# A fused two-block kernel on one core: the first stage rebuilt, top-k rounds and index pairs moved

## The reference, cut to what matters

```python
def gmlp_spatial_gating(h, w_in, ln_g, ln_b, w_s, b_s, w_out):
    uv = jax.nn.gelu(h @ w_in)                  # h is rms_norm(x); w_in 1024 x 2048
    u, v = jnp.split(uv, 2, axis=-1)
    v = layer_norm(v, ln_g, ln_b)
    v = v.reshape(bsz, nblk, 128, 8, 128)       # 4 blocks of 128 tokens, 8 channel groups
    w_masked = jnp.where(mask[None], w_s, 0)    # per group 128 x 128
    sv = jnp.einsum('gij,bnjgd->bnigd', w_masked, v)
    sv = sv + jnp.transpose(b_s)[None, None, :, :, None]
    return (u * sv.reshape(...)) @ w_out
...
    rel = jax.nn.relu(jnp.einsum('bqhd,bsd->bqhs', qib, k_idx32))     # 8 index heads
    score = jnp.einsum('bqhs,bqh->bqs', rel, wb)
    score = jnp.where(admissible[None], score, NEG_BIG)
    top_val, top_pos = lax.top_k(score, n_sel)                        # 128 of up to 512 keys
```

## Time and profile before, and how to read it

| what | value |
|---|---|
| median of 3 runs | 2488.84 us |
| profiled execution | 2489.14 us |
| its span, first to last instruction | 2487.0 us |
| PE busy | 2386.9 us (96%) |
| DVE, ACT, POOL busy | 1349.9, 811.8, 303.8 us |
| chain that ended last | PE 86%, DVE 9%, ACT 3%, issue 2% |
| one ACT pass over 128x512 fp32 | 0.63 us, with a gain 0.71 us |
| one DVE pass over 128x512 fp32 | 0.68 to 0.75 us, GpSimd silent |

### The profile page before, as it was taken

How to read it: one execution, slowest core, us unless ns; L and a number is a source line. 1 busy time by engine, 2 the same in 40 slices (tenths; PEclk the granted TensorE clock), 3 DMA queues, 4 the chain that set the end, 5 groups by cost and what they waited for, 6 DMA issues and landing times.

```text
span 2487.0 us, 28963 instructions
## 1 busy us (share of the span) xinstructions
PE 2386.9 (96%) x10924; PEld 1929.7 (78%) x10924; DVE 1349.9 (54%) x1983; ACT 811.8 (33%) x1274; POOL 303.8 (12%) x139
## 2 busy tenths in 40 slices
PE   6789999999999999999999999998999999999997
PEld 4677888887767788888788888767877888888886
DVE  5566444346566644434655445788664454444455
ACT  2113333233455433323322223330244343222233
POOL 6670000000000000000000000556540000000000
PEclk8899999999999999999999999999999999999999
DMA  4222433331223243333233333223212343333221
GB/s 171 68 85 68 119 95 99 94 101 52 75 75 100 62 124 95 93 101 98 61 100 110 93 93 94 60 68 95 67 56 62 95 130 95 107 93 102 79 79 55
DMA packets 64833, 221.94 MB, mean 89 GB/s; under 512 B 7504, under 2 KB 9680, under 8 KB 64592
## 3 DMA queue, kind: packets, MB, share of 16 engines
q1 hardware_dynamic: 59184, 208.17, 28.1%
q10 hardware_dynamic: 5536, 12.19, 1.6%
HBM read 218.23 MB, written 2.10 MB: 89 GB/s over the span
## 4 chain that ended last, share of the span: by engine, by line
PE 86%; DVE 9%; ACT 3%; issue 2%; DMA 0%; POOL 0%; ACTq 0%; DVEq 0%; POOLq 0%
PE PS L445 23%; PE PS L447 22%; PE PS L446 22%; PE PS L464 3%; PE PS L541 2%; PE PS L515 2%; PE PS L468 1%; PE PS L694 1%; DVE MK L1745 1%; PE PS L715 1%; DVE SS L1372 1%; DVE TOP L1744 1%; PE PS L704 1%; PE PS L840 1%; DVE WL L1360 1%
## 5 line engine op out<-in xcount | busy, mean ns | idle before, releaser
L445 PE MATMUL PS<-XH,WH 128*128 128x512 f32 x1632 | 647.5, 397 | 17.4 <-DVE T L1570 12.5
L447 PE MATMUL PS<-XH,WL 128*128 128x512 f32 x1632 | 637.2, 390 | 0.0
L446 PE MATMUL PS<-XL,WH 128*128 128x512 f32 x1632 | 636.8, 390 | 0.0
L1360 DVE TENSOR_TENSOR WL<-RAW,WH 128x1024 fp32r<-128x1024 f32 (+1 forms) x336 | 396.3, 1180 | 232.4 <-ACT WH L990 227.8
L990 ACT ACTIVATE WH<-RAW 128x1024 fp32r<-128x1024 f32 (+2 forms) x340 | 344.6, 1014 | 350.3 <-DVE M L1477 202.4
L445 PEld LDWEIGHTS PS<-XH,WH 128*128 128x128 f32 x1632 | 307.4, 188 | 99.4 <-issue 20.9
L445 PE MATMUL PS<-HH,WH 128*128 128x512 f32 x928 | 364.1, 392 | 2.6 <-DVE HL L1446 2.6
L447 PE MATMUL PS<-HH,WL 128*128 128x512 f32 x928 | 361.4, 389 | 0.0
L446 PE MATMUL PS<-HL,WH 128*128 128x512 f32 x928 | 361.3, 389 | 0.0
L447 PEld LDWEIGHTS PS<-XH,WL 128*128 128x128 f32 x1632 | 307.3, 188 | 65.2
L446 PEld LDWEIGHTS PS<-XL,WH 128*128 128x128 f32 x1632 | 307.8, 189 | 60.8
(11 more groups left out here) (237 smaller groups left out, 2658.2 us busy)
## 6 DMA issues: line engine op xcount, KB each, us to landing
RAW<-in_weights SPq DMA_DIRECT2D x379, 512.0 KB, 3.5
RAW<-in_weights SPq DMA_DIRECT2D x16, 384.0 KB, 3.1
H<-in_xT ACTq DMA_DIRECT2D x8, 256.0 KB, 8.6
BIAS<-in_rel ACTq DMA_DIRECT2D x8, 256.0 KB, 4.3
RAW<-in_weights SPq DMA_DIRECT2D x8, 256.0 KB, 2.6
out<-R ACTq DMA_DIRECT2D x8, 256.0 KB, 2.2
BIAS<-in_rel ACTq DMA_DIRECT2D x8, 224.0 KB, 4.6
DECAY<-in_decay ACTq DMA_DIRECT2D x1, 1024.0 KB, 4.8
```

The costliest lines, as they stand in the source:

```text
L445: nc.tensor.matmul(PS[:, bank_, :], high[:, w], xh[:, k, :], start=(k == 0), stop=False)
L446: nc.tensor.matmul(PS[:, bank_, :], high[:, w], xl[:, k, :], start=False, stop=False)
L447: return nc.tensor.matmul(PS[:, bank_, :], low[:, w], xh[:, k, :], start=False, stop=stop)
L1360: V.tensor_tensor(low[:, 0:w], RAW[:, slot, 0:w], high[:, 0:w].bitcast(F32), ALU.subtract).then_inc(weights_split, 1)
```

## The change

In the first stage:
- SP's queue carries x too: x tile 0, unit 0, x 1 and 2, unit 1, x 3 and 4, unit 2, x 5 and 6, unit 3, x 7. ACT waits for the gains alone (`in_gain`) and makes one small operation at once; BS and WST are issued from ACT at t = 4; LNG and LNB are gone, and their values come as columns of COL.
- GpSimd splits only units 256 to 294. ACT and DVE split units 0 to 27 by hand-placed calls. `WIDE` begins at unit 0, so eight slots.
- gmlp_v: the second half uses banks 4 to 7. Gelu reads PSUM with 1/rms as its scale and frees the bank itself. The normalization is one ACT pass with scale and bias per token tile; ln_g and ln_b move behind the spatial product: `gate` computes (product x ln_g + bias') x u, and bias' = ln_b x row sums of the masked w_s + b_s, the row sums being two new products with ONES (`row_sums`).
- PE's order is gate unit 0, row sums, units 1, 2, spatial 0 and 1, unit 3, spatial 2 and 3, unit 4, 4 and 5, unit 5, 6 and 7, units 6, 7, then gmlp_out. Its operands are GH and GL instead of XH and XL, and the branch result goes to M0.

In the heads: `transpose_avw` at j = 3 and index pairs from j = 3 on; relus run two further before each half swap; four instead of two adds between cosine and sine; the swapped halves of the first five heads go to PSUM banks 4 and 6; two of the four ROT products move behind the first heads. Of the 48 rounds 4 now stand in the last two heads, 16 in ret_qk, 12 in front of token_major(0), 9 in front of token_major(1), and 4 and 3 in retention heads 0 and 1.

```diff
-POOL_RANGES = ((0, 28), (256, 295))
+POOL_RANGES = ((256, 295),)
-WIDE = ((20, 96, 16), (116, 256, 112))
+WIDE = ((0, 96, 0), (116, 256, 112))
...
+                        if u == 0:
+                            for t in ((0,), (1, 2), (3, 4), (5, 6))[s]:
+                                sp.dma_start(H[:, t, :], xT[:, t, :]).then_inc(in_x[t], 16)
...
+            for f in range(DT):
+                gate_unit(f)
+                if f == 0:
+                    row_sums()
+                if 2 <= f < 6:
+                    spatial(2 * f - 4)
+                    spatial(2 * f - 3)
+            out = FIRST["gmlp_out"]
+            for k in range(DT):
+                pe.wait_ge(x_ready, DT + k + 1)
+                for u in range(out, out + 3):
+                    out_pass(u, k)
...
-                if j == 1:
+                if j == 3:
                     transpose_avw()
-                if j % 2 == 1 and j // 2 < TT * PAIRS:
-                    index_pair(j // 2)
+                if j % 2 == 1 and 0 <= j // 2 - 1 < TT * PAIRS:
+                    index_pair(j // 2 - 1)
...
+            def gelu_values(half):
+                act.wait_ge(units_done, (half + 1) * SLOTS + SLOTS)
+                for j in range(TT):
+                    S.activation(VT[:, j, half * SEQ:half * SEQ + SEQ], PS[:, half * 4 + j, :],
+                                 ACT.Gelu_apprx_tanh, scale=RT[:, TT + j:TT + j + 1]).then_inc(evacuated, 1)
...
+            for j in range(TT):
+                S.activation(VT[:, j, :], VT[:, j, :], ACT.Identity, bias=NMX[:, j:j + 1],
+                             scale=RSD[:, j:j + 1]).then_inc(v_normed, 1)
...
-            take(24, 15)
+            take(20, 12)
             token_major(0, VT)
-            take(39, 9)
+            take(32, 9)
             token_major(1, VT)
...
                 two_bank_unit(rg0 + 2 * h, GT[:, 2 * h % 4, :])
+                if h < 2:
+                    take((41, 45)[h], (4, 3)[h])
                 mask(h)
                 ret_norm(h)
```

More of the change, by code:

```diff
@@ L603, in keep_busy, with first_half @@
                     nc.tensor.matmul(PS[:, bank_, :], XH[:, 0, 0:P], XH[:, k % DT, :], start=True, stop=True)
[L605 to L613, removed]
+            def first_half():
+                for k in range(DT):
+                    q, w = k // 2, slice(k % 2 * SEQ, k % 2 * SEQ + SEQ)
+                    high, low = weights_of(q)
+                    if k == DT - 1:
+                        stat()
+                    pe.wait_ge(high_split, q + 1)
+                    pe.wait_ge(xh_ready, k + 1)
+                    for x, wt in (XH, high), (XL, high), (XH, low):
+                        if x is XL:
+                            pe.wait_ge(x_ready, k + 1)
+                        if wt is low:
+                            pe.wait_ge(weights_split, q + 1 + SLOTS)
+                        for j in range(TT):
+                            last = nc.tensor.matmul(PS[:, j, :], x[:, k, j * P:j * P + P], wt[:, w],
+                                                    start=(k == 0 and x is XH and wt is high),
+                                                    stop=(k == DT - 1 and wt is low))
+                    if k % 2 == 1:
+                        last.then_inc(units_done, 1)
@@ L968, in _ @@
             sp_ = Count(spread_ready)
-            for dst, src in ((GAIN, gains), (COL, cols), (IDENT, ident_d)):
+            act.dma_start(GAIN[:], gains).then_inc(in_gain, 16)
+            for dst, src in ((COL, cols), (IDENT, ident_d)):
                 act.dma_start(dst[:], src).then_inc(in_const, 16)
[L972 to L976, removed]
             def passed():
@@ L1102, in _ @@
[L1102 to L1105, removed]
+                S.activation(R1[:, f, :], T[:, f % 2, :], ACT.Gelu_apprx_tanh).then_inc(act_out, 1)
+                if f < 7:
+                    for u in ((14,), (15,), (16, 17), (18,), (19,), (20,), (21,))[f]:
+                        split_high(u)
+                if f == 6:
+                    act.wait_ge(gate_done, DT)
+                    for g in range(3):
+                        gated_high(g)
@@ L1106, in _ @@
+            for g in range(3, DT):
+                if g == DT - 1:
+                    split_high(22)
+                gated_high(g)
+            split_high(23)
+            ta.n = 2 + DT
+            branch_squares(FIRST["gmlp_out"], m=M0)
             branch_root()
@@ L1212, in relus @@
                      .then_inc(relu_done, 1)
-            relus(0, 10)
+            relus(0, 12)
             for t in range(TT):
@@ L1537, in half_step @@
                         split_low(u + t - 1 + AHEAD)
-            dve.wait_ge(in_const, 48)
+            dve.wait_ge(in_gain, 16)
             for t in range(DT):
[L1541 to L1545, removed]
-                for j in range(TT):
[L1547 to L1550, removed]
+                low_part(t, G_MIX0, XH, XL, x_ready)
+                if t % 2 == 0:
+                    split_low(t // 2)
+                add_square(t == 0)
@@ L1558, in _ @@
-            V.memset(WST[CH:P, :, 0:CH], 0.0)
             dve.wait_ge(act_out, ao.next())
             link(V.reciprocal(RSD[:], SD[:]))
-            for j in range(TT):
-                v = VT[:, j, :]
-                link(V.tensor_scalar(v, v, MV[:, j, 0:1], RSD[:, j:j + 1], ALU.subtract, ALU.mult))
-                link(V.tensor_tensor(v, v, LNG[:], ALU.mult))
-                last = V.tensor_tensor(v, v, LNB[:], ALU.add)
-            last.then_inc(v_normed, 1)
-            for f in range(DT):
-                if f >= 4:
-                    dve.wait_ge(act_out, ao.next())
-                V.tensor_tensor(T[:, f % 4, :], unit(), RI[:], ALU.mult).then_inc(evacuated, 1)
```

250 lines of the change are left out of this document (194 added, 56 removed).

## The result

The kernel takes **2422.25 us** (median of 4 runs, 2421.59 to 2426.27) against 2488.2 (4 runs beside it, 2483.42 to 2489.11): ratio 0.974, 95% interval 0.972 to 0.976. I had forecast 2424 and faster. The profiled execution took 2421.59 us, its span 2419.8.

The account below looks back on a forecast made before the run. PE was taken as the bound nearly everywhere, except for waits in the first stage and beside the top-k rounds. 2489.14 - 51 (first stage) - 13.5 (heads net) = 2424.6, about 2424 us; range 2414 to 2440.

Parts of the forecast that it names:

- First stage: Start to last gmlp_out unit: PE's terms sum to 149.9 us against 200.76, 51 us less.
- The cover there: First stage: v_normed ready at 65 us, first spatial group at 71.7; 6 to 7 us of cover, so no wait.
- Heads: Heads and top-k: of 15.7 us of waits 3.1 remain, plus 5 for cold starts; 17.5 us less, bounds 8 and 20.
- 4.9 us, since four adds lie between cosine and sine: Heads: index pairs' wait for relu falls from 4.9 us to 1.0, bounds 0 and 4.
- the sum would lose the 4.9 us term: Heads: if GpSimd still blocks two-input adds, only the five PSUM swaps are freed; 9 to 10 us net.
- The largest term, the rounds: Heads: moving top-k rounds cuts ret_v bank waits from 4.0 to about 1.0 us and from 2.9 to 0.5.
- The price in the retention: Retention heads 0 and 1: rounds before ret_norm make PE wait 2.5 and 1.5 us; 4 us back, between 3 and 7.
- A: First stage: DVE or ACT becomes the bound, four hand-overs late; 10.6 us back, 2435; chance 0.17.
- B: Heads give nearly nothing because GpSimd still disturbs the adds; 2 us net, 2436; chance 0.13.
- D: First stage: splitting loses its lead, each unit exposes 5.7 us; slower, about 2562; chance 0.02.
- E: First stage: x and weights on one queue land slower; 4 us back, 2429; chance 0.60 together with the forecast.
- C: Whole kernel at its good bounds: start 5.6, heads 20 less, 3 back; 2420 or a bit lower; chance 0.07.

Follow-up runs that it names:

- e5: Changed kernel with all eight spatial groups in one row behind the gate units, and gates, high and low parts behind them; 2431.7 us.
- e8: Changed kernel with 20 extra, unused ScalarE copies in front of the v normalization; 2430.48 us.
- e4: Changed kernel with GpSimd again splitting units 0 to 27; 2440.85 us.
- e6: Changed kernel with the eight x tiles issued from ScalarE's queue again instead of SP's; 2428.23 us.
- e11: Changed kernel with relus to 10 and two adds between cosine and sine, as before; index pairs stay from j = 3; 2421.38 us.
- e10: Changed kernel with the swapped halves of the first five heads back in T (SBUF) instead of PSUM banks; 2431.11 us.
- e3: Changed kernel with the seven rounds back: 19 in front of token_major(0), 9 in front of token_major(1), none in the retention loop; 2433.18 us.
- e9: Changed kernel with the four rounds of the last two ret_qk steps moved in front of token_major(0), 16 there; 2425.33 us.
- e13: Changed kernel without rounds in the last two ret_qk units, 13 in front of token_major(0) and 12 in front of token_major(1); 2420.41 us.
- e12: Changed kernel with two of the nine rounds in front of token_major(1) moved into retention head 2, before its mask; 2425.13 us.

## Why the prediction was right, and where it was not

**First stage: right as a sum.** 149.9 forecast, 149.77 measured. The terms, from the chain of after (start, us, what, count):

```profile
6.64 20.73 PE PS L635 x84
27.37 0.79 PE PS L576 x8
```

Start 6.64 (6.5). The first half, 96 matmuls and the statistics, ends at 31.04 and takes 24.40; less 21.76 and 0.79 the cold start cost 1.85 (2.3). Each pair of spatial groups takes 1.78 on PE, 7.1 in all (7.0); statistics and spreading 0.79 + 0.89 (1.75), the row sums 1.72 (1.75). No term is off by over 0.5 us. What a cold start costs differs between executions: in e5 the same first half took 0.95 us longer, which makes it 2.8.

**The cover there: right.** v_normed at 64.7 (65), wanted at 71.66 (71.7), and e8 shows that the 7.0 us are real. DVE's low parts of x stand at the 0.75 us that the earlier trace rows has with GpSimd silent (mean ns of one, whole first stage):

```profile
L1522 DVE SCALAR_TENSOR_TENSOR XL<-H,GAIN,XH 128x512 fp32r<-128x512 f32 x8 | 6.0, 744 | 5.2 <-ACT XH L1192 5.2
```

That the silence is the condition was said, its size not; e4 shows it at 20 us of the 51. The parts undone in e4, e5 and e6 cost 20.3, 9.3 and 6.1 us against after. They don't add up to 51 and need not: the norm on ScalarE and gelu from PSUM were not undone alone.

**Heads: 15.6 us against 17.5, with three steps wrong inside.** Of the waits I had 3.1 left; it is 4.5. What remains beside the waits, 15.6 - 11.2 = 4.4 us, I put down to the cold starts (5 forecast): before has granted clocks of 0.91, 0.95, 0.97 and 0.91 over 1630 to 1650 and in the three stretches of 20 us from 1680 to 1740, after has 1.00 throughout.
- The step "4.9 us, since four adds lie between cosine and sine" failed. e11 undoes just that, brings back 2.4 us of relu wait and loses nothing. From 1550 to 1650 us DVE is the bound, with 92 of 100 us busy in after; the waits of PE there are one debt shown at several places. I summed them as if each had a cause of its own.
- The step on the Trainium skill, "SBUF — State Buffer", Who interferes with whom, that by its rule "the sum would lose the 4.9 us term", failed too, though the rule itself agrees with every row: two DVE operations with two SBUF inputs take 2.87 and 2.38 us beside GpSimd in e4, the swaps in PSUM stay at 0.69. The rule says who is held up. Which wait is paid with it, it can't say. In e10 the places of the five swaps, to which I had given no term, are worth about 6 us, more than anything else in the heads but the rounds.
- The largest term, the rounds, was half right. At token_major(0) 4.0 us fell to 1.0 as forecast, and e3 shows that the seven moved rounds are worth 10.9 us now. At the first ret_v half I had 2.9 fall to 0.5, and it fell to 2.2: the last four rounds in ret_qk still stand in front of that bank. e9 and e13 take them out, and the wait is gone.

**The price in the retention: wrong, 0 instead of 4 us.** PE waits at no transpose of the loop. The step that failed is "four rounds are 6.1 us; 3.5 us of slack; PE waits 2.5". The rows of after:

```profile
1693.79 1.90 DVE L1990 TENSOR_SCALAR YN<-PS,MV,RSD 128x256 f32<-128x256 f32 x4
...
1696.20 1.04 PE L956 MATMUL PS<-IDENT,YN 128*128 128x128 f32 x8
```

From the gate unit to the first YN it is 9.35 us, where the kernel before has 6.64: 2.7 us more for 6.1 us of rounds, and that fits into the slack of 3.5. The missing 3.4 us are the mask's: its two passes start 0.61 us behind the gate unit before and take 1.41 and 2.40 us there too. In head 1 it is the same, 7.18 us before and 8.43 after for 4.6 us of rounds, within the slack of 3.0. I added rounds to a row of DVE and took all other operations at the duration that they had at their old time. The mask was stretched by its time and not by its work. The Trainium skill, "SBUF — State Buffer", Who interferes with whom, also says that tensor_scalar in its two-port mode takes the port that GpSimd needs, and the trace agrees (1.41 and 2.40 us against 0.23), though it does not name the mode in which the mask ran; I had read that rule for two inputs only.

The errors cancel in part: 17.5 - 4 = 13.5 forecast, 15.6 - 0 measured. That the total lies 2 us from the forecast is in part luck, and 0.6 us of the gain are clock in code that did not change.

**The rivals.** A (a bound inside the first stage), B (the heads give nothing), D (slower) and E did not happen. C (start 5.6, heads 20 less, 3 back, 2420) was nearer on the net of the heads than my forecast, 15.6 against 17 and 13.5, though not by its reasons.

## What to carry to other kernels

Where one engine is the bound over a stretch, as DVE is here in the heads, treat the waits of the other as one debt: count the bound's busy time and take work out of the stretch; a reordering that removes a named wait may only move it on, as e11's did. Look for the bound's idle time behind the next hand-over (6.8 us here), and move work there. Before an operation is priced at the duration its row shows, ask what ran beside it then, and whether it will after the move.

## What the runs showed of the hardware

- An operation of DVE with two SBUF inputs, or a tensor_scalar or copy from SBUF to SBUF, that starts beside a split of GpSimd ends 0.1 to 0.6 us after GpSimd's operation does (e3, e4, e10, e12), and that is its own duration less 0.14 us: 0.55 us for the additions of 0.69 in e4 and e10, 0.28 for a copy of 0.42 in e4, 0.09 for the passes of 0.23 in e3. So it goes as if it began when GpSimd is done, and its price is the rest of the other's operation and not a factor: 0.23 us became 1.41 and 2.40, 0.69 became 2.38. MAX8, MATCH_REPLACE8 and operations with one of their inputs in PSUM kept their 0.7 us.
- After the same wait, PE was at times granted the lower clock and at times not: 2.16 us in after with 1.00 over the ten microseconds around it, 2.13 us in e12 with 0.83. In e12 the heads are 1.5 us longer for it. The spread between runs of one kernel goes with the clock too: three runs of after at 2421.59 to 2422.31 us have a mean granted clock of 0.991, the fourth, at 2426.27, has 0.989, and 0.002 of 2420 us is about 4.8 us.
